# Cached value pages in visits of four pages, and a reordered start, in a one-core decoder step

## The reference, cut to what matters

```python
xn = rms_norm(x, norm_w)                                  # mean of squares over all 1024 channels
aq, ak, av, az, mq, mk, mv, mo, mz, ga, gm, mi, mf = jnp.split(xn @ w_in, points, axis=-1)
...
# a sample: 8 pages of keys and of values, [128 tokens, 8 heads, 128]
gate = einsum(q, mean of keys over a block)               # top 3 of 4 blocks
p = softmax(concatenate([q . k_selected * scale, q . k_new * scale]))
out = p_selected @ v_selected + p_new * v_new
...
h = rms_norm(h.reshape(B, S, ML_HEADS, ML_HD), mh_norm_w) # per mLSTM head
y = x + (sigmoid(ga) * y_att + sigmoid(gm) * y_ml) @ w_out
```

## Time and profile before

| | |
|---|---|
| median of three runs | 481.1 us |
| profiled execution | 482.34 us, span 480.2 us |
| TensorE busy | 462.4 us (96%) |
| VectorE busy | 403.8 us (84%) |
| ScalarE busy | 290.0 us (60%) |
| chain that ended last | TensorE 72%, VectorE 19%, DMA 3%, issue 3%, ScalarE 2% |
| HBM traffic | 313 GB/s over the span |

### The profile page before, as it was taken

How to read it: one execution, slowest core, us unless ns; L and a number is a source line. 1 busy time by engine, 2 the same in 40 slices (tenths; PEclk the granted TensorE clock), 3 DMA queues, 4 the chain that set the end, 5 groups by cost and what they waited for, 6 DMA issues and landing times.

```text
span 480.2 us, 11312 instructions
## 1 busy us (share of the span) xinstructions
PE 462.4 (96%) x3848; PEld 420.8 (88%) x3848; DVE 403.8 (84%) x1650; ACT 290.0 (60%) x486; POOL 101.3 (21%) x181
## 2 busy tenths in 40 slices
PE   3899999999989999989999999999999999999997
PEld 2699899898879899889899989989889898999997
DVE  2878899789999898999999999979999973577861
ACT  2776555586884485785665595558757458234430
POOL 2031312112323221532322242222223110000000
PEclk9999999999999999999999999999999999999999
DMA  8399489748799999999999999998999996546521
GB/s 315 149 351 365 145 324 332 259 158 311 230 415 418 408 364 332 328 380 415 415 404 329 377 404 394 412 393 308 339 420 407 417 413 250 176 155 238 186 85 46
DMA packets 36377, 150.86 MB, mean 314 GB/s; under 512 B 5200, under 2 KB 6740, under 8 KB 29024
## 3 DMA queue, kind: packets, MB, share of 16 engines
q1 hardware_dynamic: 12160, 70.77, 38.8%
q0 software_dynamic: 19008, 67.20, 36.5%
q10 hardware_dynamic: 5152, 12.18, 6.5%
HBM read 137.37 MB, written 12.76 MB: 313 GB/s over the span
## 4 chain that ended last, share of the span: by engine, by line
PE 72%; DVE 19%; DMA 3%; issue 3%; ACT 2%; ACTq 0%; DVEq 0%
PE pj L515 28%; PE pj L518 14%; PE wk L515 8%; DVE w L1037 5%; DVE kpages L1144 4%; PE pa L708 4%; PE wk L518 4%; DVE cslot L1230 4%; DMA out_C_s<-cslot 2%; PE wk L482 2%; PE wk L620 2%; PE wk L652 1%; PE pa L494 1%; PE wk L523 1%; PE wk L524 1%
## 5 line engine op out<-in xcount | busy, mean ns | idle before, releaser
L515 PE MATMUL pj<-xn,w 128*128 128x264 f32 x1344 | 183.2, 289 | 2.9 <-ACT mqT L946 2.9
L515 PEld LDWEIGHTS pj<-xn,w 128*128 128x128 f32 x1344 | 170.6, 189 | 11.5 <-issue 6.8
L1037 DVE TENSOR_TENSOR w<-wraw,w 128x1024 fp32r<-128x1024 f32 x112 | 136.9, 1225 | 10.9 <-ACT w L792 10.4
L792 ACT ACTIVATE w<-wraw 128x1024 fp32r<-128x1024 f32 x112 | 117.8, 1053 | 27.6 <-PE wk L518 12.8
L1144 DVE CUSTOM_DVE_ANT_0 kpages<-kpages,qbc 128x128 f32<-128x128 f32 x512 | 114.6, 286 | 3.4 <-DMA kpages<-in_cache_k 3.3
L518 PE MATMUL pj<-xn,w 128*128 128x264 f32 x672 | 95.4, 284 | 1.6 <-DVE w L1037 1.6
L518 PEld LDWEIGHTS pj<-xn,w 128*128 128x128 f32 x672 | 86.5, 188 | 2.3 <-DVE w L1037 2.2
L399 POOL DMA_DIRECT2D kpages<-in_cache_k x64 | 34.3, 536 | 180.6 <-DVE sco L1144 152.5
L399 POOL DMA_DIRECT2D vpages<-in_cache_v x64 | 33.9, 530 | 67.4 <-issue 39.0
L1144 DVE DVE_READ_ACCUMULATOR2_ANT sco<- 128x1 f32 x512 | 40.5, 79 | 0.0
L708 PE MATMUL pa<-vpages,prob 128*32 128x256 f32 x512 | 34.3, 385 | 0.8 <-ACT prob L851 0.8
(11 more groups left out here) (269 smaller groups left out, 637.8 us busy)
## 6 DMA issues: line engine op xcount, KB each, us to landing
wraw<-in_weights SPq DMA_DIRECT2D x56, 1024.0 KB, 8.0
kpages<-in_cache_k POOLq DMA_DIRECT2D x64, 512.0 KB, 8.5
vpages<-in_cache_v POOLq DMA_DIRECT2D x64, 512.0 KB, 10.6
cslot<-in_states SPq DMA_DIRECT2D x16, 512.0 KB, 11.0
out_C_s<-cslot ACTq DMA_DIRECT2D x16, 512.0 KB, 8.5
xres<-in_tokens SPq DMA_DIRECT2D x1, 1056.0 KB, 7.5
out_k_p<-kT ACTq DMA_DIRECT2D x4, 256.0 KB, 11.8
out_v_p<-v_nat ACTq DMA_DIRECT2D x4, 256.0 KB, 6.3
```

The lines of the kernel that those rows point to most:

```text
L515: mm(bank[:, 0:T], w2[:, q, 0, k, :], src[:, g, k, :], start=(k == 0 and g == 0), stop=False)
L792: A(w2[:, n % WSPLIT, 0], wraw[:, pair % WRAW, :, (n % 2) * P:(n % 2 + 1) * P], ACT.Copy).then_inc(whi_ready, 1)
L1037: V.tensor_tensor(w2[:, q, 1], wraw[:, slot, :, half * P:(half + 1) * P], w2[:, q, 0], ALU.subtract).then_inc(wlo_ready, 1)
```

## The change

It has four parts. The value pages are visited four at a time, at lags 14 and 18, and GpSimd asks for the pages that follow one chunk later than the visit, after that chunk's key page. The start has four token transfers instead of two, six matmuls on zeros ahead of the first sum (`BLANKS`), the token norms in one row before the low parts, and a first projection whose three passes wait for less each. The mLSTM norm has its own tile `mrs`, and `mlg_ready` is no longer waited for by ScalarE at i = 2 and 4 but by VectorE before `rope_norm`. Two memsets of VectorE move behind the low parts.

```diff
+BLANKS = 6
-SUMS, SELECT, SHIFT, EXP, VALUES, TOTAL, GATHER, COLUMNS, OUT = 9, 10, 11, 12, 13, 15, 20, 21, 22
+SUMS, SELECT, SHIFT, EXP, VALUES, TOTAL, GATHER, COLUMNS, OUT = 9, 10, 11, 12, 14, 15, 20, 21, 22
+VPAGES = 4
-def value_pair(g):
-    for p in range(PAGES // 2):
-        b = due(g, VALUES + 2 * p)
+def value_pages(g):
+    for p in range(0, PAGES, VPAGES):
+        b = due(g, VALUES + p)
...
# GpSimd, after keys(s + KSLOTS) of chunk g
-                pair = value_pair(g)
-                if pair is not None:
-                    for s in range(pair[0] * PAGES + 2 * pair[1] + VSLOTS, pair[0] * PAGES + 2 * pair[1] + VSLOTS + 2):
-                        if s < NB * PAGES:
-                            values(s)
+                used = value_pages(g - 1)
+                if used is not None:
+                    first = used[0] * PAGES + used[1] + VSLOTS
+                    for s in range(first, min(first + VPAGES, NB * PAGES)):
+                        values(s)
# SyncE and ScalarE queues: tokens
-            sp.dma_start(xT[:, 0:4, :]..., a["tokens"][:, 0:4 * T]).then_inc(boot_x[0], 16)
+            for part in (0, 2):
+                sp.dma_start(xT[:, 2 * part:2 * part + 2, :]..., ...).then_inc(boot_x[part], 16)
# TensorE, first
+            pe.wait_ge(blank, 3)
+            for _ in range(BLANKS):
+                mm(wk[3][:, 0:NB * VC], qmask[:, 0, 0:P], qmask[:, 0, :], start=True, stop=True)
# TensorE, first projection
+                if parts:
+                    for k in range(KC):
+                        pe.wait_ge(xhi_ready, k // 2 + 1)
+                        mm(bank[:, 0:T], w2[:, q, 0, k, :], src[:, 0, k, :], start=(k == 0), stop=False)
+                    pe.wait_ge(wlo_ready, n + 1)
+                    for k in range(KC):
+                        mm(bank[:, 0:T], w2[:, q, 1, k, :], src[:, 0, k, :], start=False, stop=False)
+                    for k in range(KC):
+                        pe.wait_ge(parts, k + 1)
+                        last = mm(bank[:, 0:T], w2[:, q, 0, k, :], src[:, 1, k, :], start=False, stop=(k == KC - 1))
# TensorE, values
-                    for pg in (2 * pair[1], 2 * pair[1] + 1):
+                    for pg in range(turn[1], turn[1] + VPAGES):
# ScalarE: split_hi(0) ahead of the high parts of the tokens; the norm's tile
-                act.wait_ge(kT_ready, 2 * j + 2)
-                inv_rms(wk[3][:, 0:T], rs[:, 0, :], MHD).then_inc(mrs_ready, 1)
+                act.wait_ge(mlg_ready, j)
+                inv_rms(wk[3][:, 0:T], mrs[:, :], MHD).then_inc(mrs_ready, 1)
...
-                    act.wait_ge(mlg_ready, j)
+                    act.wait_ge(kT_ready, 2 * j)
# VectorE: squares and sums part by part; after the eight norms
-                if k in (3, 5):
-                    dve.wait_ge(xn_ready, k - 1)
-                    x_lo(k // 2 - 1)
+            split_lo(0)
             dve.wait_ge(xn_ready, KC)
-            x_lo(2)
-            x_lo(3)
-            split_lo(0)
+            for p in range(KC // 2):
+                x_lo(p)
```

More of the change, by code:

```diff
@@ L222, in build @@
         rsum = sb("rsum", [P, 2, 2])
+        mrs = sb("mrs", [P, T])
         pj = [ctx.enter_context(nc.psum_tensor(f"pj{i}", [P, 512], F32)) for i in range(2)]
@@ L271, in build @@
         boot, boot_c, boot_r, boot_n, boot_g = sem("boot"), sem("boot_c"), sem("boot_r"), sem("boot_n"), sem("boot_g")
-        boot_x = [sem(f"boot_x{i}") for i in range(2)]
+        boot_x = [sem(f"boot_x{i}") for i in range(4)]
         blank, blank_eye = sem("blank"), sem("blank_eye")
@@ L338, in load_queries @@
                 load_w(n)
-            sp.dma_start(xT[:, 0:4, :].rearrange("p k t -> p (k t)"), a["tokens"][:, 0:4 * T]).then_inc(boot_x[0], 16)
+            for part in (0, 2):
+                sp.dma_start(xT[:, 2 * part:2 * part + 2, :].rearrange("p k t -> p (k t)"),
+                             a["tokens"][:, 2 * part * T:2 * (part + 1) * T]).then_inc(boot_x[part], 16)
             sp.dma_start(cst[:, 0:C_FIRST], a["consts"][:, 0:C_FIRST]).then_inc(boot_c, 16)
@@ L509, in project @@
                     return
+                if parts:
[8 more added lines that the diff above has]
+                        last = mm(bank[:, 0:T], w2[:, q, 0, k, :], src[:, 1, k, :], start=False, stop=(k == KC - 1))
+                    last.then_inc(proj, 1)
+                    return
                 for k in range(KC):
-                    if parts:
-                        pe.wait_ge(parts, k + 1)
                     for g in range(2):
@@ L696, in cache_side @@
                     mm(page_sums[b % 2], ones, prob[:, b % 2, 0:PAGES * HEADS], start=True, stop=True).then_inc(l_ps, 1)
[L697 to L700, removed]
+                turn = value_pages(g)
+                if turn is not None:
+                    b = turn[0]
+                    if turn[1] == 0:
                         pe.wait_ge(prob_ready, b + 1)
                         pe.wait_ge(accr_ready, b)
-                    for pg in (2 * pair[1], 2 * pair[1] + 1):
+                    for pg in range(turn[1], turn[1] + VPAGES):
                         s = b * PAGES + pg
@@ L774, in _ @@
             act.sem_inc(mrs_ready, 1)
-            act.dma_start(xT[:, 4:8, :].rearrange("p k t -> p (k t)"), a["tokens"][:, 4 * T:8 * T]).then_inc(boot_x[1], 16)
+            for part in (1, 3):
+                act.dma_start(xT[:, 2 * part:2 * part + 2, :].rearrange("p k t -> p (k t)"),
+                              a["tokens"][:, 2 * part * T:2 * (part + 1) * T]).then_inc(boot_x[part], 16)
             nc.scalar.preload_act_table_set("natural_log_exp_and_others")
             for half in range(2):
-                act.wait_ge(boot_x[half], 16)
+                act.wait_ge(boot_x[2 * half], 16)
                 part = slice(4 * half, 4 * half + 2)
@@ L792, in split_hi @@
                 A(w2[:, n % WSPLIT, 0], wraw[:, pair % WRAW, :, (n % 2) * P:(n % 2 + 1) * P], ACT.Copy).then_inc(whi_ready, 1)
+            split_hi(0)
             for p in range(KC // 2):
-                if p == 1:
-                    split_hi(0)
                 act.wait_ge(xn_ready, 2 * p + 2)
@@ L1040, in _ @@
             for half in range(2):
-                dve.wait_ge(boot_x[half], 16)
+                dve.wait_ge(boot_x[2 * half + 1], 16)
                 part = slice(4 * half + 2, 4 * half + 4)
-                ch.step(V.tensor_tensor(xsq[:, part], xT[:, part], xT[:, part], ALU.mult))
-            ch.join()
-            for half in range(2):
+                ch.link(V.tensor_tensor(xsq[:, part], xT[:, part], xT[:, part], ALU.mult))
                 dve.wait_ge(xsq_act, half + 1)
-                part = slice(4 * half + 2, 4 * half + 4)
                 V.tensor_tensor(xsq[:, part], xsq[:, part], xsq[:, 4 * half:4 * half + 2], ALU.add).then_inc(xsq_dve, 1)
-            dve.wait_ge(blank, 6)
-            ch.step(V.memset(gpad[:, NBLK:, :], 3.0e38))
-            ch.step(V.memset(pairs[:, :, 0:NBLK - 1, :], 0.0))
             dve.wait_ge(boot, 16)
@@ L1068, in _ @@
                                        op0=ALU.mult, op1=ALU.mult).then_inc(xn_ready, 1)
-                if k in (3, 5):
-                    dve.wait_ge(xn_ready, k - 1)
-                    x_lo(k // 2 - 1)
+            split_lo(0)
             dve.wait_ge(xn_ready, KC)
-            x_lo(2)
-            x_lo(3)
-            split_lo(0)
+            for p in range(KC // 2):
+                x_lo(p)
+            dve.wait_ge(blank, 6)
+            ch.step(V.memset(gpad[:, NBLK:, :], 3.0e38))
+            ch.step(V.memset(pairs[:, :, 0:NBLK - 1, :], 0.0))
             dve.wait_ge(gate_raw, 2)
@@ L1194, in keys_side @@
                     dve.wait_ge(rs_ready, HEADS + 2 * j + n + 1)
+                    dve.wait_ge(mlg_ready, j)
                     rope_norm(kT[:, n, :], rs[:, n, :], wk[2 * n + 1], kT_ready)
@@ L1307, in round_close @@
                 for e in range(EC):
-                    ch.step(V.scalar_tensor_tensor(out=hT[:, e, :], in0=hT[:, e, :], scalar=mhw[:, e:e + 1], in1=rs[:, 0, :],
+                    ch.step(V.scalar_tensor_tensor(out=hT[:, e, :], in0=hT[:, e, :], scalar=mhw[:, e:e + 1], in1=mrs[:, :],
                                                    op0=ALU.mult, op1=ALU.mult))
```

## The result

The changed kernel takes 497.6 us, the median of four runs (497.28 to 500.4). The kernel before took 481.67 beside it (480.91 to 483.06). The ratio is 1.033 with an interval of 1.030 to 1.037, so the change costs 15.9 us. The forecast of 486 had the sign and not the size; the time lies above the range.

What follows compares the result with a forecast made beforehand. TensorE, VectorE and the DMA engines were all taken as nearly full. Terms -3.4 - 4.0 - 2.9 + 11.9 + 2.9 = +4.5 us on the median of 481.1 gave 486 us, range 472 to 496.

Steps and rivals of the forecast that it cites:

- The start: Before the first projection: earlier token sums at a raised clock gain 4.0 us, or 1.8 at the low clock.
- Fewer visits: TensorE's value visits: four pages each gain 1.9 us in the tail and 1.5 in the body, together 3.4.
- The tile `mrs`: Start of second and third rounds: its own tile removes TensorE's waits for ScalarE's copy, 2.9 us at most.
- low weights late next: At those round starts: `mrs` gains 0 if VectorE's low weights are late next; the forecast took 2.9 us.
- The price of the later requests: GpSimd's value requests: late pages cost TensorE 11.9 us, plus 2.9 as the `mrs` gain is lost there.
- The waits for value pages: Second visits of samples 0, 2 and 5: TensorE waits 2.9, 3.9 and 5.1 us; samples 1, 3, 4 none.
- Keys late as well: Rival, GpSimd's queue: four value pages delay the next keys, VectorE waits for them; 496 us, chance 0.16.
- The rival's own point: Key pages: this rival decides once a key takes over some 16 us from request to landing.
- Pages in time: Rival, value transfers: a calmer queue lands critical pages within 6 us, no visit waits; 471 to 475 us, chance 0.30.
- A balance: Rival, whole kernel: waits of 8 to 12 us cancel the gains, time within 0.5%; chance 0.14.
- its bound of 22.4 us: Second visits of samples 0, 2 and 5: upper bound of page waits, late by 6.5, 7.1 and 8.8 us.
- The blanks: Start: six blank matmuls raise TensorE's clock; the rival that they don't gives 488 us, without its own chance.

Runs made afterwards that it cites:

- eight slots: The changed kernel with eight value slots instead of six and three key slots instead of four; 497.99 us, ratio 1.032.
- the filled wait: The changed kernel with useless matmuls ahead of the two late value pages of sample 5; 495.92 us, ratio 1.031.
- the split requests: The changed kernel with two of the four pages asked for in the visit's chunk and two a chunk later; 483.41 us, ratio 1.003.
- the pairs: The changed kernel with value visits of two pages and requests in the visit's own chunk, as before the change; 476.55 us, ratio 0.990.
- the run of the values alone: The kernel before with only the visits of four and their later requests; 502.17 us, ratio 1.040.
- resident values: The changed kernel with only the first six value pages loaded and used by all visits of four; 476.59 us, ratio 0.989.

## Why the prediction was right or wrong

**The start** was right: 4.65 us against 4.0, the first projection at 14.1 to 17.2, and mostly by the clock.

**Fewer visits** was right as work and wrong as time. The pieces of 1.86 us are there, and TensorE has 2.8 us less to do (predicted 3.4). But the forecast counted the body's 1.5 in full beside a VectorE that was busy 262.5 of 282 us. With no value page late the body lost 2.7 us instead of gaining: TensorE came early, waited more for VectorE and ScalarE, and lost its clock behind the wait of 2.35 us.

**The tile `mrs`** was worth 1.3 and not 2.9: the case "low weights late next", which the forecast named and didn't take.

**The price of the later requests** is the step that failed: the sum took it as TensorE's own waits for value pages, 11.9 us, and put at nothing what the four requests do to the transfers behind them and to the clock. The runs showed 8.9 us of such waits, 9.8 more of waits for VectorE's low weights, and a left-over of 7.1 taken for matmuls at 1.2 GHz.

**The waits for value pages** that the sum did have are there, and where the forecast looked for them: at the second visit. The sizes were read from a queue as full as before. Forecast and measured: sample 0, 2.9 and 0.55; sample 2, 3.9 and 0; sample 5, 5.1 and 7.4; samples 1, 3, 4 together 0 and 0.92. In samples 0 and 2 the late pages landed in 6.2 to 6.8 us, and not in the 8.8 and 10.7 that the earlier trace rows less 2.7 gave, the queue being emptier, as I read it: value pages now land in 8.9 us (median over the run) and keys in 7.1, before 10.6 and 8.5. The sum of the page waits, 8.9 against 11.9, is near by luck: of the three waits one came at 0.55 us, one not at all, and the third was 7.4 for 5.1. In sample 2 two other waits (2.7 and 1.5 us up to 221.05 and 225.70) had slowed TensorE before its visit, and the page landed at 229.3, a quarter microsecond before its turn.

**What was not in the sum** was in a rival. "Keys late as well" described the burst ahead of the next keys and gave it 0.16. In GpSimd's timeline of the kernel after:

```profile
195.46 0.54 POOL L404 DMA_DIRECT2D vpages<-in_cache_v  x1 [1.01 <-issue]
...
198.93 0.53 POOL L404 DMA_DIRECT2D vpages<-in_cache_v  x1 [0.62 <-issue]
...
200.27 0.56 POOL L404 DMA_DIRECT2D kpages<-in_cache_k  x1
```

and the landing of that one key page, in the view of its tile:

```profile
DMA to landing us min/median/max: 17.6/17.6/17.6
```

The rival's own point was 16 us. At the same place the kernel before had a pair ahead of the key asked for at 203.8, which landed in 11.3 us. VectorE waits for this key, and TensorE for VectorE:

```profile
217.94 0.29 DVE L1157 CUSTOM_DVE_ANT_0 kpages<-kpages,qbc 128x128 f32<-128x128 f32 x1 [3.50 <-DMA kpages<-in_cache_k]
```

```profile
221.05 1.24 PE L538 MATMUL pj<-xn,w 128*128 128x264 f32 x8 [2.69 <-DVE w L1058]
...
225.70 1.24 PE L538 MATMUL pj<-xn,w 128*128 128x264 f32 x8 [1.46 <-DVE w L1058]
```

The rival saw only keys. The burst of sample 3 hit the decay rows instead (GpSimd's timeline):

```profile
267.89 0.53 POOL L404 DMA_DIRECT2D vpages<-in_cache_v  x1 [0.64 <-issue]
269.85 0.53 POOL L404 DMA_DIRECT2D kpages<-in_cache_k  x1 [1.43 <-issue]
...
270.88 0.49 POOL L429 DMA_DIRECT2D floor<-rows_dram  x1
283.57 0.54 POOL L433 PARTITION_BROADCAST decay<-decay  x1 [12.20 <-DMA floor<-rows_dram]
```

and behind it VectorE's, then TensorE's timeline of the same kernel:

```profile
284.56 0.29 DVE L1253 TENSOR_TENSOR decay<-decay,cst 128x128 f32<-128x128 f32 x1 [4.99 <-POOL floor L434]
```

```profile
288.15 2.13 PE L538 MATMUL pj<-xn,w 128*128 128x264 f32 x8 [3.91 <-DVE w L1058]
```

Two small transfers had to wait behind four value pages and a key page. The forecast named what stands behind TensorE's waiting matmul; what stands behind the four requests in GpSimd's queue it named only in the rival, and there only the keys.

**The clock** was in no term. The forecast took a wait of TensorE as costing its own length. Here it costs that and, behind some waits, a stretch at 1.2 GHz: 7.1 us in the books, where it is what is left over, and some 2 us shown at one place by the filled wait. The sum of the rival (496) had no such term either and came near the result by its bound of 22.4 us for page waits; its number was close, its working not.

**The other rivals.** "Pages in time" fell with the waits at sample 5; with eight slots (and a key slot fewer) its premise was made true and the kernel still took 498. "A balance" fell too. The blanks did raise the clock.

Shown by runs: that the values' part costs all of it; that visits of four by themselves cost 0.5 us by the medians; that requests a chunk earlier give back 7.3 us and two and two for four in one turn another 6.8; that later requests harm even in pairs; and that the clock's fall follows the idleness. Argued only: how the 7.1 us spread over the three falls, how much of the loss is late pages and how much late keys and rows, what the last 6.9 us between the split requests and the pairs are, and why eight slots with late keys come out at just the time of after.

## What to carry to other kernels

On an in-order queue that serves several readers, count for every request what will stand behind it: asking for twice as much half as often makes the small and the urgent transfers wait longest, and four requests spread over two turns cost 6.8 us less than all four in the first of these turns. The room of a prefetch is the slots less what one visit frees, so a bigger visit on the same slots is paid for in time between request and use. A saving in the engine that leads is worth only what the engine behind it can follow; look for it in the stretch (here the tail) where that one has room.

## What the runs showed of the hardware

**The clock falls behind single waits.** In its profiled run the kernel before, with TensorE busy 277 of 282 us, has no wait of 2 us behind the start and no fall. In other runs it can: of 17 beside the last experiments four have a mean clock of 0.996 and take 484.9 to 486.7 us, the twelve at 1.000 take 480.4 to 483.5. In the traces the waits of 2.80 us and more each went with 3.4 to 10.2 us at 1.2 GHz. Shorter ones went both ways: 2.29 us in the run of the values alone was followed by a fall and 2.29 in the filled kernel was not, 2.35 with resident values was and 2.69 at 221.05 in the kernel after was not; the shortest with a fall was one of 1.71 us with eight slots. At 1.2 GHz sixteen matmuls of 264 columns took 3.84 us for 2.12.

**Time to landing goes with what stands ahead.** Pages of the same 512 KB took 17.6 us (a key asked for at 200.27) and 6.2 (a value asked for 22.8 us later) in one run, the first behind four value pages, the second behind one key and one value. It isn't four in a row alone: in the kernel before, a key asked for at 147.5, behind two pairs and two keys asked for in the ten us ahead of it, took 16.0. And 58 of 64 value transfers left out changed the time of the kernel by 0.5 us.
